# A new prologue for a hybrid attention and mLSTM layer: the order of its loads, tiles in pairs, and the low parts of h made by GpSimd

## The chip, the cores and the metric

The kernel runs on one core of one Trainium2 chip. The metric is the device time of one execution in microseconds, lower is better. The engines are TensorE (PE), VectorE (DVE), ScalarE (ACT), GpSimd (POOL) and SyncE (SP), which here only issues DMAs. Each engine runs its own instructions in order and waits on semaphores that others raise.

## The reference

One decoder layer, batch 1, sequence 1024, width 1024, all float32:

```
mod = silu(c) @ w_ada + b_ada;  shift, scale, gate = split(mod, 3)
h = x * (1 + scale) + shift
proj = h @ w_in + b_in      # 8 heads of stick-breaking attention: q k v z (4 x 512);
                            # 4 heads of mLSTM: q k v o z (5 x 512), i f (2 x 4); two merge gates (2 x 1024)
y_sb = (stick_breaking(q, k, v) * silu(z)) @ w_sb_proj
y_ml = (head_norm(mlstm(silu(conv(q, k)), v, i, log_sigmoid(f))) * sigmoid(o) * silu(z)) @ w_ml_proj
y = (sigmoid(g_sb) * y_sb + sigmoid(g_ml) * y_ml) @ w_out
out = layer_norm(alpha * x + (1 + gate) * y, ln_g, ln_b)
```

The prologue is the part that matters here: the conditioning `mod` (only shift and scale; 1024 x 2048 weights), `h`, and the first products with `w_in`.

## The kernel before, in words

h is kept transposed in SBUF: 8 tiles (d or k from 0 to 7), each of 128 channels on the partitions by 1024 tokens. To get float32 precision from the fast matmul mode (fp32r), every operand is split into a high and a low part, and a product is three matmuls: high by high, low by high and high by low (`split_product`, lines 614 to 619). So each tile of h exists as `hH` (a rounded copy) and `hL` (the rest). Weights are split in the same way, in chunks of four k tiles: ACT makes the high part (`wH` or `w_proH`) and DVE the low part (`wL` or `w_proL`).

The prologue goes over the 8 tiles, d = 0 to 7. For each tile:

- SP loads 128 columns of x (`x_rows`, line 453) and the 2 x 128 conditioning columns of `w_ada` (`a_raw`, line 457, three buffers). All loads of the prologue are on SP's one queue, in this order; the rows that they read are 512 bytes long. The small parameter rows (`prm`, seven loads) go ahead of all.
- DVE multiplies the eight 128-row blocks of `a_raw` with silu(c) and adds them up in two sums (`ada_rows`, lines 1323 to 1338: two TENSOR_SCALAR, six SCALAR_TENSOR_TENSOR, one addition, all 256 wide).
- PE sums over the partitions with two one-column matmuls by ones (`ada_columns`, line 655), and DVE adds the bias (`mod_columns`, lines 1366 and 1367): the shift and scale columns of the tile.
- PE transposes x (`turn_x`, line 667: two PSUM banks of four 128x128 transposes), ACT makes `h_raw` = x * scale + shift from the two banks (line 944) and copies it to `hH` (line 948). `h_raw` has two buffers. DVE makes `hL` = `h_raw` - `hH` (`low_h`, line 1360).
- PE multiplies the tile with the weights of jobs 0, 1 and 2 (`tile_of`): job 0 is the eight gate rows i and f (128x8 weights), in two PSUM banks; jobs 1 and 2 are q and k of the first pair of attention heads (128x128 weights). Each job is 6 matmuls of 512 columns in a tile: 2 halves of the tokens by 3 terms.

PE's order is written out by hand (lines 699 to 711): columns of tile 0; then for each d: transposes of x tile d, jobs 0 and 1 of tile d-1, columns of tile d+1, job 2 of tile d-1. After the last tile come jobs 3 and 4 (v and z of that pair), 48 matmuls each over all of h (`project`, line 639). Job 3 writes the PSUM banks of job 1, so it waits until ACT has copied jobs 0 and 1 out (`drained`). Then `gate_columns` (line 691) transposes rows made from the gates, and the main loop of four iterations begins.

Beside jobs 3 and 4 runs the chain of the gate rows. POOL zeroes four row buffers that lie where `x_rows` was (lines 563 to 567, `rows_zero`) once PE has transposed the last x. ACT copies job 0 out of PSUM with its bias to `r_if` (line 961). SP moves the rows by eight small DMAs to four partition groups (`r_f`, `r_i`, lines 470 and 472). Then ACT takes exponential and logarithm (lines 993, 995), DVE does two scans and builds `r_q` (lines 1388 to 1408), and ACT takes exponentials (line 1000). In DVE's order the low part of weight chunk 9 stands behind the scans (`row_logs`, `pro_split`).

POOL does nothing between its constants, which end at about 4 us, and the zeroing.

Of the kernel before, what the change touches and what calls it, by code (L numbers as in the profile page):

```python
# [25 lines left out]
P = 128  # L26
D = 1024
# [102 lines left out]
A_BUFS = 3  # L130
Y_BUFS = 4


# [64 lines left out]
def build_kernel(nc, x, c, w_ada, b_ada, w_in, b_in, conv_w, conv_b, ml_norm_g, w_sb_proj, w_ml_proj, w_out,  # L198
# [13 lines left out]
    with ExitStack() as ctx:  # L212
# [30 lines left out]
        next_v, next_g = lt("next_v", [P, S]), lt("next_g", [P, S])  # L243
# [39 lines left out]
        a_raw = pt("a_raw", [P, A_BUFS, KT, 2, P])  # L283
        a_acc = pt("a_acc", [P, 2, 2, 2, P])
# [3 lines left out]
        w_proH = pt("w_proH", [P, PRO_CHUNKS, 4, P], F32R)  # L288
        w_proL = pt("w_proL", [P, PRO_CHUNKS, 4, P], F32R)
# [31 lines left out]
        params_in, bias_in = sem("params_in"), sem("bias_in")  # L321
        x_cols_in = [sem(f"x_cols_in{d}") for d in range(KT)]
# [4 lines left out]
        ada_summed = sem("ada_summed")  # L327
        ada_used, ada_done, mod_done = sem("ada_used"), sem("ada_done"), sem("mod_done")
# [50 lines left out]
        pro_ps = [[y_ps[0:2 * NH, :], misc_ps[2][0:2 * NH, :]],  # L379
                  [proj_ps[half][:] for half in range(2)], [z_ps[half][:] for half in range(2)]]  # L380
        ada_ps = misc_ps[0]
# [16 lines left out]
        def banks(number):  # L398

            return z_ps if number > J_GATES and (number - J_GATES) % 2 else proj_ps  # L400

# [24 lines left out]
        def _(sp):  # L426
            bi = b_in[0]
            rows = [
                (ROW_C, c[0]), (ROW_ADA, b_ada[0]), (ROW_B, bi[0:OFF_IF]),
                (ROW_GSB, bi[OFF_GSB:OFF_GSB + 2 * D]), (ROW_CB, conv_b[0]), (ROW_NG, ml_norm_g[0]),  # L430
            ]
            for row, src in rows:
                src = src.rearrange("(t p) -> t p", p=P)
                sp.dma_start(prm[row:row + src.shape[0], :], src).then_inc(params_in, 16)
            sp.dma_start(prm[ROW_CW:ROW_CW + 4 * KT, :], conv_w[0].rearrange("j (t p) -> (j t) p", p=P))\
                .then_inc(params_in, 16)

# [13 lines left out]
            for d in range(KT):  # L451
                cols_d = slice(d * P, (d + 1) * P)
                sp.dma_start(x_rows[:, :, cols_d], x_v[:, :, cols_d]).then_inc(x_cols_in[d], 16)
                if d >= A_BUFS:
                    sp.wait_ge(ada_used, KT * (d - A_BUFS + 1))
                for what in range(2):
                    sp.dma_start(a_raw[:, d % A_BUFS, :, what], w_ada_w[:, :, what, cols_d])\  # L457
                        .then_inc(a_in[d % A_BUFS], 16)
# [1418 lines left out]
```

## Time and profile before

| | us |
|---|---|
| median of 3 runs (962.40 to 962.66) | 962.57 |
| the profiled execution's own time | 964.36 |
| its span, first to last instruction | 962.6 |
| PE busy (share of the span) | 931.1 (97%) |
| DVE busy | 616.4 (64%) |
| ACT busy | 440.4 (46%) |
| POOL busy | 165.5 (17%) |
| mean granted TensorE clock | 0.996 |

PE is the busy engine, and the chain that ended last lies on PE for 89% of the span. Matmuls are pipelined, so that a busy PE isn't PE at its peak; the record of a matmul is longer than the distance between two. Idle time of the other engines costs nothing by itself. The first 24 us are the only stretch in which PE is idle for long: its busy share is 2 tenths in the first of the page's 40 slices, and 9 or more in all the others.

### The profile page before, as it was taken

What the parts mean: (1) busy time and instruction counts of PE and PEld (TensorE: products, weight loads), DVE (VectorE), ACT (ScalarE), POOL (GpSimd) and SP (SyncE); (2) the same over time, 40 slices, a digit from 0 to 9 for tenths busy, and PEclk for the clock granted to TensorE, in tenths of its full rate; (3) what the DMA queues carried; (4) which work ended last, traced back from release to release, by engine and by line L of the source; (5) the groups of instructions that cost most, each with busy time, mean ns of one, the idle gap of its engine ahead of it and who ended that gap; (6) DMA issues with size and microseconds to landing.
All of it is one profiled execution on the core that took longest, in us unless ns stands there. A gap on an engine that the chain in (4) does not pass through costs nothing.

```text
span 962.6 us, 12901 instructions
## 1 busy us (share of the span) xinstructions
PE 931.1 (97%) x4965; PEld 759.7 (79%) x4965; DVE 616.4 (64%) x1112; ACT 440.4 (46%) x717; POOL 165.5 (17%) x114
## 2 busy tenths in 40 slices
PE   2999999999999999999999999999999999999996
PEld 1677878888878888788888888888888888878885
DVE  4756886755976647976649967534653333345996
ACT  2454566553666544575544665425743222242100
POOL 1010232220223230322311322211100000001200
PEclk9999999999999999999999999999999999999999
DMA  9941211112201022111112111127612212215232
GB/s 228 291 99 48 67 35 39 35 36 67 77 23 45 23 55 78 43 45 34 33 44 89 33 35 34 43 55 237 211 45 67 53 46 53 88 44 186 91 129 87
DMA packets 99560, 73.95 MB, mean 77 GB/s; under 512 B 4616, under 2 KB 90760, under 8 KB 99500
## 3 DMA queue, kind: packets, MB, share of 16 engines
q1 hardware_dynamic: 94828, 58.44, 22.7%
q0 software_dynamic: 2368, 8.41, 2.6%
q10 hardware_dynamic: 2304, 6.29, 1.8%
q8 instruction: 39, 0.64, 0.3%
q14 instruction: 21, 0.17, 0.1%
HBM read 64.59 MB, written 8.40 MB: 76 GB/s over the span
## 4 chain that ended last, share of the span: by engine, by line
PE 89%; DVE 4%; ACT 2%; SPq 2%; DMA 2%; issue 1%; DVEq 0%; ACTq 0%
PE bank L639 44%; PE bank L619 10%; PE bank L617 10%; PE bank L618 10%; PE bank L758 4%; PE bank L746 3%; PE bank L733 2%; DMA a_raw<-in_w_ada 2%; PE bank L716 2%; DVE rem L1503 1%; PE bank L735 1%; PE bank L734 1%; SPq L457 1%; PE bank L781 1%; PE bank L783 1%
## 5 line engine op out<-in xcount | busy, mean ns | idle before, releaser
L639 PE MATMUL bank<-hH,wH 128*128 128x512 f32 x688 | 271.1, 394 | 0.6 <-DVE wL L1343 0.6
L639 PE MATMUL bank<-hL,wH 128*128 128x512 f32 x688 | 271.2, 394 | 0.0
L639 PE MATMUL bank<-hH,wL 128*128 128x512 f32 x688 | 271.1, 394 | 0.0
L577 POOL TENSOR_TENSOR ez<-ez,rem 128x512 f32<-128x512 f32 x72 | 134.5, 1881 | 396.8 <-DVE rem L1503 396.8
L1343 DVE SCALAR_TENSOR_TENSOR wL<-w_raw,wH 128x512 fp32r<-128x512 f32 x116 | 99.3, 860 | 109.2 <-ACT wH L920 107.9
L639 PEld LDWEIGHTS bank<-hH,wH 128*128 128x128 f32 x688 | 129.3, 188 | 30.3 <-DVE wL L1343 2.1
L639 PEld LDWEIGHTS bank<-hH,wL 128*128 128x128 f32 x688 | 129.3, 188 | 28.8 <-issue 2.9
L639 PEld LDWEIGHTS bank<-hL,wH 128*128 128x128 f32 x688 | 129.2, 188 | 28.8 <-issue 2.9
L1503 DVE TENSOR_TENSOR_SCAN rem<-rem,ones 128x512 f32<-128x512 f32 (+2 forms) x96 | 99.9, 1093 | 35.1 <-ACT rem L1020 35.1
L920 ACT ACTIVATE wH<-w_raw 128x512 fp32r<-128x512 f32 x116 | 72.5, 627 | 104.3 <-PE bank L619 71.1
L1008 ACT ACTIVATE ez<-bank 128x512 f32<-128x512 f32 x72 | 39.1, 596 | 101.1 <-PE bank L735 101.1
L618 PE MATMUL bank<-hL,wH 128*128 128x512 f32 x144 | 56.2, 390 | 0.0
L617 PE MATMUL bank<-hH,wH 128*128 128x512 f32 x144 | 56.2, 390 | 0.0
L619 PE MATMUL bank<-hH,wL 128*128 128x512 f32 x144 | 56.0, 389 | 0.0
L606 POOL TENSOR_TENSOR yL<-yT,yH 128x1024 fp32r<-128x1024 f32 x4 | 9.6, 2402 | 207.5 <-ACT yH L1272 207.5
L1016 ACT ACTIVATE rem<-ez 128x512 f32<-128x512 f32 x72 | 41.4, 625 | 7.7 <-DVE y_stage L1510 6.1
L1020 ACT ACTIVATE rem<-rem 128x512 f32<-128x512 f32 x72 | 41.1, 621 | 0.0
L1027 ACT ACTIVATE at<-bank 128x512 f32<-128x512 f32 x72 | 38.7, 592 | 3.3 <-PE bank L746 3.3
L617 PE MATMUL bank<-hH,yH 128*128 128x512 f32 x96 | 38.5, 401 | 0.0
L618 PE MATMUL bank<-hL,yH 128*128 128x512 f32 x96 | 38.1, 396 | 0.0
L619 PE MATMUL bank<-hH,yL 128*128 128x512 f32 x96 | 38.0, 396 | 0.0
L746 PE MATMUL bank<-ident,ez 128*128 128x128 f32 x288 | 37.2, 272 | 0.0
(241 smaller groups left out, 1499.6 us busy)
## 6 DMA issues: line engine op xcount, KB each, us to landing
w_raw<-in_w_in SPq DMA_DIRECT2D x104, 256.0 KB, 2.9
a_raw<-in_w_ada SPq DMA_DIRECT2D x16, 512.0 KB, 7.3
x_rows<-in_x SPq DMA_DIRECT2D x8, 512.0 KB, 6.4
raw<-in_w_ada POOLq DMA_DIRECT2D x8, 512.0 KB, 4.8
x_in<-in_x SPq DMA_DIRECT2D x8, 512.0 KB, 4.2
out_y<-res SPq DMA_DIRECT2D x7, 512.0 KB, 2.9
raw<-in_w_out SPq DMA_DIRECT2D x10, 256.0 KB, 4.5
m_w<-bm_scratch ACTq DMA_DIRECT2D x4, 512.0 KB, 3.5
```

The source lines that it names most:

```text
L577: g.tensor_tensor(e, e, r, ALU.mult).then_inc(a_done[h], 1)
L617: t.matmul(ps, aH, bH, start=k == 0, stop=False)
L618: t.matmul(ps, aH, bL, start=False, stop=False)
L619: return t.matmul(ps, aL, bH, start=False, stop=k == kt - 1)
L639: ins = t.matmul(banks(number)[half][:], w, a, start=(r == 0), stop=(r == JOB_MM // 2 - 1))
L746: ins = t.transpose(z_ps[h][:, b * P:(b + 1) * P], ez[s % 2][h][:, b * P:(b + 1) * P], ident[:])
L920: a.activation(wH[:, slot, :, 0:width], w_raw[:, slot, :, 0:width], ACT.Copy, scale=scale)\
L1008: a.activation(ez[s % 2][h][:], z_ps[h][:], ACT.Exp).then_inc(ex_done[h], 1)
L1016: a.activation(rem[s % 2][h][:], ez[s % 2][h][:], ACT.Ln, bias=1.0).then_inc(ln_done[h], 1)
L1020: a.activation(r, r, ACT.Exp, scale=-1.0).then_inc(rem_done[h], 1)
L1343: v.scalar_tensor_tensor(out=wL[:, slot, :, 0:width], in0=w_raw[:, slot, :, 0:width], scalar=scale, in1=wH[:, slot, :, 0:width], op0=ALU.m ...
L1503: v.tensor_tensor_scan(back, back, ones[:, 0:1].to_broadcast((P, hi - lo)), first, ALU.mult, ALU.min).then_inc(scan_done[h], 1)
```

## The change

It touches the prologue alone, up to the copies of job 0 and the moves of its rows.

1. **Loads.** SP loads c and b_ada first, then the conditioning weights ahead of x. The tiles are in blocks [0], [1], [2, 3], [4, 5], [6, 7]: a block of two is loaded with rows of 1 KB, its weights in two pieces of four k blocks each. There are four buffers for pieces (`A_BUFS`), the fourth where `next_v` and `next_g` lie. The other parameter rows are loaded from ACT's queue, ahead of its table load. Weight chunks 3 to 5 are loaded after block 2.
2. **Conditioning.** DVE's row products are 512 wide for a block of two. Of its eight, ACT makes the first two (`ada_begin`), after the first tile of the block before (d = 0, 2, 4). PE makes all columns of the block at once, between jobs 1 and 2 of the tile ahead of the block, and DVE adds the bias to all in one instruction (the 1 is added to the scale's bias once).
3. **Turning x.** PE transposes x two tiles ahead: tile d+2 at the end of tile d. `ada_ps` moves to another bank, so that it no longer shares one with the transposes.
4. **Gate rows.** Job 0 is done in full float32, from `h_raw` and the raw weights, as two matmuls for each tile instead of six. Its two halves write partitions 0 to 7 and 32 to 39 of one PSUM bank, so they lie in different column groups of the array.
5. **Low parts of h.** `low_h` is on POOL, all eight before the zeroing.
6. **After the last tile.** ACT copies half 0 of job 0 with its bias; DVE copies half 1 from partitions 32 to 39 to its place (`if_moved`), and ACT adds the bias there. The four moves to `r_i` are issued from ACT's queue behind that, ahead of the copies of jobs 1 and 2; those to `r_f` stay on SP.

```diff
@@ SP
+            for b, tiles in enumerate(BLOCKS):
+                cols_b = slice(tiles[0] * P, (tiles[-1] + 1) * P)
+                for number, lo, hi in ada_pieces(b):
+                    if number >= A_BUFS:
+                        sp.wait_ge(ada_used, ada_freed(number))
+                    for what in range(2):
+                        sp.dma_start(ada_piece(number, lo, hi)[:, :, what], w_ada_w[:, lo:hi, what, cols_b])\
+                            .then_inc(a_in[number % A_BUFS], 16)
+                sp.dma_start(x_rows[:, :, cols_b], x_v[:, :, cols_b]).then_inc(x_cols_in[b], 16)
+                for g in {0: range(3), 2: range(3, PRO_CHUNKS)}.get(b, ()):
+                    pro_load(g)
...
-            for q in range(4):
-                sp.dma_start(r_i[32 * q:32 * q + NH, :], r_if[0:NH, :]).then_inc(rows_in, 16)
@@ POOL
+            def low_h(d):
+                pool.wait_ge(hH_done, d + 1)
+                g.tensor_tensor(hL[:, d], h_raw[:, d % 2], hH[:, d], ALU.subtract).then_inc(hL_done, 1)
+
+            for d in range(KT):
+                low_h(d)
             pool.wait_ge(m_filled[0], KT + 1)
             pool.wait_ge(m_filled[1], KT)
             for z in (r_i, r_f, r_if):
@@ PE
+            def gate_rows(d):
+                for n in range(2):
+                    pe.wait_ge(m_drained[n], d + 2 - n)
+                if d % 4 == 0:
+                    pe.wait_ge(wL_done, PRO_K * (d // 4) + 1)
+                for half in range(2):
+                    ins = t.matmul(pro_ps[0][half], w_if[:, d], h_raw[:, d % 2, halves(half)], start=d == 0,
+                                   stop=d == KT - 1, skip_group_check=True)
...
+            turn_x(0)
             ada_columns(0)
+            turn_x(1)
             for d in range(KT):
...
+                gate_rows(d)
+                tile_of(d, 1)
+                if d + 1 < KT and BLOCKS[BLOCK_OF[d + 1]][0] == d + 1:
+                    ada_columns(BLOCK_OF[d + 1])
+                tile_of(d, 2)
+                if d + 2 < KT:
+                    turn_x(d + 2)
@@ ACT
             def shifted(d):
-                act.wait_ge(mod_done, 2 * d + 2)
+                act.wait_ge(mod_done, BLOCK_OF[d] + 1)
                 if d > 1:
+                    act.wait_ge(if_used, d - 1)
                     act.wait_ge(hL_done, d - 1)
...
+            def ada_begin(b):
+                act.wait_ge(a_in[ada_pieces(b)[0][0] % A_BUFS], 32 * (ada_pieces(b)[0][0] // A_BUFS + 1))
+                act.wait_ge(silu_done, 1)
+                act.wait_ge(ada_done, b - 1)
+                for k in range(ada_first(b)):
+                    a.activation(ada_sum(b, k), ada_row(b, k), ACT.Copy, scale=silu_c[:, k:k + 1]).then_inc(ada_begun, 1)
...
             for d in range(KT):
                 shifted(d)
-                if d < 3:
-                    pro_split(d + 3)
+                if d in (0, 2, 4):
+                    ada_begin(d // 2 + 2)
+                if d == 3:
+                    for g in range(3, PRO_CHUNKS):
+                        pro_split(g)
...
+                if n == 0:
+                    for half in range(2):
+                        act.wait_ge(drained[half], 1)
+                    for q in range(4):
+                        act.dma_start(r_i[32 * q:32 * q + NH, :], r_if[0:NH, :]).then_inc(rows_in, 16)
@@ DVE
+            other_columns()
+            ada_rows(0, 0, KT)
+            mod_columns(0)
+            for g in range(3):
+                pro_split(g)
+            for b in range(1, len(BLOCKS)):
+                ada_rows(b, 0, KT // 2)
+                ada_rows(b, KT // 2, KT)
+                mod_columns(b)
+                if b == 3:
+                    for g in range(3, PRO_CHUNKS):
                         pro_split(g)
-            low_h(KT - 1)
+            dve.wait_ge(filled[1], 1)
+            dve.wait_ge(rows_zero, 5)
+            v.tensor_copy(r_if[0:2 * NH, halves(1)], pro_ps[0][1]).then_inc(if_moved, 1)
             for g in range(PRO_CHUNKS, PRO_CHUNKS + 3):
                 pro_split(g)
```

## Rows read from the trace of the kernel before

**Rows 1.** The page: busy us of the engines, share of the span, instructions

```profile
PE 931.1 (97%) x4965; PEld 759.7 (79%) x4965; DVE 616.4 (64%) x1112; ACT 440.4 (46%) x717; POOL 165.5 (17%) x114
```

**Rows 2.** Stretches: length, PE, PEld, DVE, ACT, POOL busy; clock, DMA share, GB/s

```profile
45.00:50.00 5.00, 5.00 (x23) 3.30 (x22) 3.77 (x11) 2.61 (x3) 0.00 (x0) 0.79 1.14 291
...
55.00:60.00 5.00, 5.00 (x27) 3.67 (x27) 4.17 (x13) 2.51 (x3) 0.00 (x0) 1.00 0.06 17
```

**Rows 3.** Timeline of DVE, 0 to 62 us: start, length, instruction, idle before

```profile
11.43 0.61 DVE L1331 TENSOR_SCALAR a_acc<-a_raw,silu_c 128x256 f32<-128x256 f32 x2 [4.28 <-DMA a_raw<-in_w_ada]
...
16.05 0.15 DVE L1367 SCALAR_TENSOR_TENSOR mod<-bank,cols 128x1 f32<-128x1 f32 x1
...
23.32 0.15 DVE L1367 SCALAR_TENSOR_TENSOR mod<-bank,cols 128x1 f32<-128x1 f32 x1
...
55.45 0.15 DVE L1367 SCALAR_TENSOR_TENSOR mod<-bank,cols 128x1 f32<-128x1 f32 x1
...
60.96 0.15 DVE L1367 SCALAR_TENSOR_TENSOR mod<-bank,cols 128x1 f32<-128x1 f32 x1
```

**Rows 4.** Timelines of DVE, POOL, ACT, SP and PE, 60 to 77 us

```profile
65.26 1.23 DVE L1360 TENSOR_TENSOR hL<-h_raw,hH 128x1024 fp32r<-128x1024 f32 x1 [4.15 <-ACT hH L948]
...
63.08 0.95 POOL L564 MEMSET r_i<- 128x1024 f32 x1 [58.30 <-PE bank L667]
...
66.77 0.11 POOL L567 MEMSET r_one<- 128x8 f32 x1
...
67.94 1.28 ACT L961 ACTIVATE r_if<-bank,r_bias 8x512 f32<-8x512 f32 x2 [1.16 <-PE bank L619]
...
76.09 1.06 ACT L993 ACTIVATE r_e<-r_f 128x1024 f32<-128x1024 f32 x1 [4.05 <-DMA r_i<-r_if]
...
69.33 2.55 SPq L470 DMA_DIRECT2D r_f<-r_if  x4
...
71.15 0.39 PE L639 MATMUL bank<-hH,wH 128*128 128x512 f32 x1
```

**Rows 5.** PE's timeline at 85.5 us, and the chain that ended last, there

```profile
85.52 0.50 PE L639 MATMUL bank<-hH,wH 128*128 128x512 f32 x1 [0.58 <-DVE wL L1343]
...
85.52 8.48 PE bank L639 x36
```

**Rows 6.** Timeline of SP's DMA issues: the first load of x

```profile
3.48 0.43 SPq L453 DMA_DIRECT2D x_rows<-in_x  x1
```

**Rows 7.** Timeline of PE around its pause at 41 us, and later

```profile
41.82 0.61 PE L655 MATMUL bank<-ones,a_acc 128*128 128x1 f32 x4 [1.52 <-DVE a_acc L1337]
...
43.86 1.91 PE L667 MATMUL bank<-ident,x_rows 128*128 128x128 f32 x8
...
46.42 0.63 PE L619 MATMUL bank<-hH,w_proL 128*8 128x512 f32 x1
...
50.89 1.04 PE L667 MATMUL bank<-ident,x_rows 128*128 128x128 f32 x8
```

**Rows 8.** Groups, 0 to 72 us: shapes, count, busy us, mean ns, idle before

```profile
L944 ACT ACTIVATE h_raw<-bank,mod 128x512 f32<-128x512 f32 x16 | 11.9, 776 | 29.0 <-PE bank L667 29.0
...
L948 ACT ACTIVATE hH<-h_raw 128x1024 fp32r<-128x1024 f32 x8 | 8.5, 1061 | 0.7
...
L1352 DVE SCALAR_TENSOR_TENSOR w_proL<-w_raw,w_proH 128x512 fp32r<-128x512 f32 x4 | 2.6, 682 | 0.0
```

**Rows 9.** Line 606 on POOL: ns min/median/max, first and last start

```profile
L606 POOL TENSOR_TENSOR yL<-yT,yH x4: 2400/2402/2403, 875.7 to 909.7; 128x1024 fp32r<-128x1024 f32 x4
```

**Rows 10.** Timeline of POOL and DVE around 188 us

```profile
187.64 3.87 POOL L577 TENSOR_TENSOR ez<-ez,rem 128x512 f32<-128x512 f32 x2 [9.08 <-DVE rem L1503]
...
188.65 1.71 DVE L1343 SCALAR_TENSOR_TENSOR wL<-w_raw,wH 128x512 fp32r<-128x512 f32 x1
```

**Rows 11.** Timeline of PE: full float32 matmuls (each recorded twice)

```profile
862.99 1.88 PE L877 MATMUL bank<-g_acc,ones 128*128 128x512 f32 x4
...
130.68 1.09 PE L758 MATMUL bank<-at,v_tok 128*64 128x128 f32 x16
```

More of the change, by code:

```diff
@@ L129, with pro_slot, ada_pieces, ada_first @@
 PRO_CHUNKS = 2 * PRO_K
-A_BUFS = 3
+A_BUFS = 4
+BLOCKS = [[0], [1], [2, 3], [4, 5], [6, 7]]
+BLOCK_OF = [b for b, tiles in enumerate(BLOCKS) for _ in tiles]
 Y_BUFS = 4
+def pro_slot(g):
+    return (g // PRO_K) * (PRO_K - 1) + g % PRO_K - 1
+def ada_pieces(b):
+    if b < 2:
+        return [(b, 0, KT)]
+    return [(2 * b - 2 + part, part * KT // 2, (part + 1) * KT // 2) for part in range(2)]
+def ada_first(b):
+    return 0 if b < 2 else 2
+def ada_steps(b, k):
+    return sum(KT - ada_first(x) for x in range(b)) + max(k - ada_first(b), 0)
+def ada_freed(number):
+    return [ada_steps(b, hi) for b in range(len(BLOCKS)) for n, _, hi in ada_pieces(b) if n == number - A_BUFS][0]
 def segments():
@@ L426, in _ @@
         def _(sp):
[L427 to L436, printed above, removed]
+            sp.dma_start(prm[ROW_C:ROW_C + KT, :], c[0].rearrange("(t p) -> t p", p=P)).then_inc(c_in, 16)
+            sp.dma_start(prm[ROW_ADA:ROW_ADA + 3 * KT, :], b_ada[0].rearrange("(t p) -> t p", p=P)).then_inc(c_in, 16)
             def load(slot, src, split):
@@ L979, in _ @@
                             act.wait_ge(rows_zero, 5)
-                        bias_copy(r_if[0:2 * NH, halves(half)], half, n,
-                                  r_bias[0:2 * NH, :], pro_ps[0][half])
+                        else:
+                            act.wait_ge(if_moved, 1)
+                        rows = r_if[0:2 * NH, halves(half)]
+                        bias_copy(rows, half, n, r_bias[0:2 * NH, :], rows if half else pro_ps[0][half])
                     elif n < 4:
@@ L1370, in _, with mod_columns @@
-            for d in range(KT):
-                ada_rows(d)
-                if d:
-                    low_h(d - 1)
-                mod_columns(d)
-                if d == 0:
-                    for g in range(3):
+            def mod_columns(b):
+                dve.wait_ge(ada_done, b + 1)
+                first, tiles = BLOCKS[b][0], len(BLOCKS[b])
+                bias = cols[:, ROW_ADA:ROW_ADA + 2 * KT].rearrange("p (w d) -> p w d", w=2)[:, :, first:first + tiles]
+                v.tensor_tensor(mod[:, :, first:first + tiles],
+                                ada_ps[:, 0:2 * tiles].rearrange("p (w d) -> p w d", w=2), bias, ALU.add)\
+                    .then_inc(mod_done, 1)
```

180 lines of the change are left out of this document (96 added, 84 removed).

## The prediction

> **What bounds the kernel now.** I read the page first: TensorE (PE) is busy for 931.1 of 962.6 us [rows 1]. So a change can gain only in the 31 us in which PE idles or runs at its lower clock, and the prologue holds most of them. Next, the table by stretches: the transfers run at 291 GB/s from 45 to 50 us and have ended by 55 (17 GB/s), the granted clock is 0.79 between 45 and 50 us, and PE is full by then [rows 2]. Third, VectorE's (DVE's) timeline: the conditioning columns of the first tile of h exist at 16.2 us, and those of the last two tiles come at 55.6 and 61.1, 5.51 us apart [rows 3]. That interval is PE's own work for one tile, since PE has no gap there. Fourth, the end of the prologue [rows 4]: hL of tile 7 is ready at 66.5, the zeroing on GpSimd (POOL) ran from 63.08 to 66.88, before the gate rows were there, ScalarE (ACT) copies them out from 67.94, and PE goes on without a gap to job 3 at 71.15. Last, the only later stall that the prologue causes: PE waits 0.58 us at 85.5 for weights whose low part stands behind the scans on DVE; and 36 matmuls in 8.48 us make 0.236 us for each [rows 5].
>
> So the number that counts is the start of job 3, now 71.15. After it come 22 us of pure projection, with the row chain beside them, and none of that changes in length.
>
> **The start.** The conditioning weights are issued at about 1.6 us, behind two small parameter loads of 0.4 each, instead of at 3.9 behind seven and 512 KB of x [rows 6]. Before, 1.5 MiB issued from 3.48 were there at 11.43: 7.9 us, of which 5.4 are transfer at 290 GB/s and 2.5 latency. Now 1 MiB from 1.6 takes 3.6 + 2.5, so it is there at 7.7. The columns exist 4.8 us after the landing (11.43 to 16.20 [rows 3]): 12.5 instead of 16.2. The parameter rows, now on ACT's queue, land by then; nothing waits for them.
>
> **The first two tiles.** Tile 1's weights have 3 MiB in all before them: 1.6 + 2.5 + 10.8 = 14.9, and its x is there at 16.7. PE turns that x before it does tile 0 (1.9 us at the low clock [rows 7]), then the gate rows (1.0), one 128-column part of tile 0 (six matmuls: 1.4 at full clock, 2.6 at the low one) and the columns (1.0, and 0.2 for DVE): 22.2 to 23.5. Today they come at 23.5 [rows 3]. The early start is used up here.
>
> **The step for one tile.** ACT makes h_raw in two pieces and hH: two of 0.72 or so, and 1.06, 2.5 us [rows 8]. POOL makes hL. The nearest operation is POOL's subtraction of the same shape, 2.40 us [rows 9]; DVE did it in 1.23 [rows 4]. After it PE does a part (1.4 to 2.6), then the next columns (0.7 to 1.4 with DVE's sum). So the columns of pair 2, 3 come 7.0 to 8.9 us after those of tile 1: 29.2 to 32.4.
>
> **The cadence of a pair.** The next pair's columns stand on PE behind the part of the second tile of this pair. By that way a pair costs h_raw and hH (2.5), the two first products that ACT now makes between the two tiles (512 wide, half of hH's 1.06 and a start-up: about 2 x 0.6), h_raw and hH again (2.5), hL (2.4), the part (1.4), columns (0.8), and some 0.4 for semaphores: 11.2 us. Today two tiles cost 2 x 5.51 = 11.0. The pairs make DVE cheaper (one operation of 0.68 [rows 8] for two narrower ones), but DVE isn't what sets this chain: hL, ACT's extra products and PE's order are in it.
>
> A second way is longer if POOL and DVE can't work at once. In the trace a DVE operation that takes 0.68 us elsewhere [rows 8] takes 1.71 when it is issued beside POOL's [rows 10]. DVE then starts its products when hL of the first tile is done, 5.0 us after the columns, needs 6 x 0.66 + 0.7 = 4.7, stands once more for 2.4, and the columns take 0.8: 12.9 us. The Trainium skill (SBUF — State Buffer, "SBUF: two separate sides") says why: the port pair is "an exclusive lock, not a bandwidth split", and a DVE operation with two SBUF inputs wants it. By that rule the pair costs 12.9, without it 11.2; rows 10 agree with the rule. I take 12.1 for each of the two pairs, between the ends, because the second stand may fall where DVE has already finished.
>
> **The end of h.** After the last pair's columns come 2.5 + 2.5 on ACT and 2.4 on POOL, 7.6 with semaphores. hL of tile 7 is then ready at 29.2 + 22.4 + 7.6 = 59.2 at best and 32.4 + 25.8 + 7.6 = 65.8 at worst, or 68 if PE's pauses keep the clock low for much of the time. I take 64.5. That is only 2 us before today's 66.5. Faster transfers don't help: even at 290 GB/s the last piece, the 13th MiB after 1.6, is there at about 51, when the chain wants it near 52. Wider rows can only bring it earlier.
>
> **The gate rows.** Six fast matmuls become two in full float32. Two such matmuls of 512 columns took 1.88 us to the end of the last, and eight of 128 columns that alternate between halves of the array's columns took 1.09 [rows 11]; the first is the bound if they run one after the other, the second, scaled by four quarters of a pair (some 1.0), if side by side. The skill (TensorEngine Tiling (Array Packing), "Key Properties") says that tiles work in parallel; by that 1.0 instead of 1.4, else 1.7. Either is hidden while the chain waits for ACT and POOL, but for up to 0.7 us at the end. I take 1.0.
>
> **What stands behind the last hL.** This is where I expect the loss. POOL does all eight hL first and zeroes its rows only then. The zeroing takes 3.8 us (63.08 to 66.88 [rows 4]) and was hidden; now it begins at the end of hL 7. Behind it stand, one after the other: ACT's copy of one half of the gate rows (0.65; DVE moves the other beside it), ACT's bias on the other (0.65), four DMA issues that this ACT queue now makes (SP made four such in 2.55 [rows 4]; at 0.43 each, as for x [rows 6], 1.7), and the copy of job 1's first half (0.65). Only then may job 3 write its bank. That is 8.3 us, or 7.5 with quick issues. Job 3 thus starts at 64.5 + 8.3 = 72.8, against 71.15: +1.65.
>
> PE has finished tile 7 by 68.3 (hL at 64.5, with the gate row and 2.8 us behind it) and stands for some 4 us. After a pause of 1.5 us today's clock fell for a while: eight transposes took 1.91 instead of 1.04, and matmuls 0.63 us instead of the usual 0.40 until about 47 [rows 4, 7]. That pause cost 0.87 + 4 x 0.23 = 1.8 us, and I put nearly the same on job 3: +1.7 (from 0 to 2.4).
>
> **The row chain.** The moves to r_f wait on SP behind the load of chunk 9, which waits for a split behind DVE's new copy: issued at hL + 5.5, landed at hL + 10.4 = 74.9, while ACT began on them at 76.09 today [rows 4]. It gains 1.2 while PE loses 3.3, so the 0.58 stall goes: -0.6. Nothing else becomes late; the transposed gate columns follow 17 us after that landing, at 92, and PE wants them at 97.
>
> **Sum.** +1.65 + 1.7 - 0.6 = +2.75. The profiled execution took 964.36, 1.8 more than the median shown, so 967.1 for such an execution and **965.3** against the median 962.57.
>
> **Rivals.**
> (a) *Neutral, 0.25.* The clock doesn't fall, or hL 7 comes at 62.5: job 3 at 70.8 + 1.7 - 0.6, so 963.3.
> (b) *Faster, 0.2.* The place is the chain of pairs: at 11.2 us, with pair 2, 3 at 29.2, hL 7 is there at 59.2 and job 3 at 67.5. That is -3.65 - 0.6 + 1.7 = -2.55, 960.0 (958.3 without the clock's part). For it speaks that PE, DVE and the transfers all have room; against it, the low clock and rows 10. It decides from hL 7 before 59.9: at 61.8 the change breaks even, at 59.9 it gains 0.2%.
> (c) *The lock decides, 0.2.* Both pairs at 12.9 and low clock in most pauses: hL 7 at 67.5, job 3 at 75.8, +4.65 + 1.7 - 0.6: 968.3. The skill's exclusive lock alone gives 65.8 and 966.6.
> (d) *It doesn't do what it says, 0.02.* POOL's hL takes over 3 us, as its 512-wide multiplications beside DVE took 1.9 each [rows 10] and not half of 2.4: over 970.
>
> The forecast itself has 0.33, between 964.5 and 967. A measurement of this kernel can tell 0.2% (1.9 us) from no change. Faster by more than that: (b), 0.2. Within: (a) and a little of the forecast, 0.27. Slower: 0.53. The range from 959.5 to 969.5 leaves out the ends of (b) and of (c) with (d).
>
> **What would show it.** Right: columns of tile 0 at 12.4 and of the last pair at 52 to 58; pairs 11 to 13 us apart; the zeroing straight behind the last hL; PE idle 3 to 5 us ahead of L639's first matmul, released by ACT's next_q copy, and a granted clock below 1 there; no wait for wL at job 4. Wrong: hL 7 before 60, or job 3 without a gap behind tile 7, or a DVE that isn't slowed beside POOL.

## The result: 967.4 us, 5.0 us slower

| | before | after |
|---|---|---|
| median (us) | 962.40 (962.27 to 962.66, 5 runs) | 967.36 (967.34 to 971.06, 5 runs) |
| the profiled execution, and its span | 964.36, 962.6 | 967.36, 965.6 |

The ratio of the means is 1.0062, 95% interval 1.0046 to 1.0078 (so are the ratios below). The forecast was 965.3 (959.5 to 969.5), slower the likeliest with 0.53; the measured time lies in that range, and just outside the band of 964.5 to 967 in which the forecast itself was to hold. In the profiled executions the span grew by 3.0 us, and my sum said 2.75; the rest of the difference lies in the profile of before, as will be shown.

The busy time of the page, the line that answers to [rows 1]:

```profile
PE 930.6 (96%) x4950; PEld 756.2 (78%) x4950; DVE 612.5 (63%) x1061; ACT 443.5 (46%) x723; POOL 185.5 (19%) x122
```

PE does the same work as before. POOL has 20 us more: eight low parts of 2.3 to 2.8. DVE has only 4 us less, although it gave up eight low parts of 1.23. Its timeline says why; it answers to [rows 3] (start, length, instruction; in brackets the idle time before it and who ended it):

```profile
12.64 0.16 DVE L1462 TENSOR_TENSOR mod<-bank,cols 128x2 f32<-128x2 f32 x1 [1.11 <-PE bank L699]
23.53 0.16 DVE L1462 TENSOR_TENSOR mod<-bank,cols 128x2 f32<-128x2 f32 x1 [2.94 <-PE bank L699]
31.78 0.16 DVE L1462 TENSOR_TENSOR mod<-bank,cols 128x4 f32<-128x4 f32 x1 [1.27 <-PE bank L699]
35.32 7.67 DVE L1432 SCALAR_TENSOR_TENSOR a_acc<-a_raw,silu_c,a_acc 128x512 f32<-128x512 f32 x6 [3.38 <-ACT a_acc L1023]
44.86 0.16 DVE L1462 TENSOR_TENSOR mod<-bank,cols 128x4 f32<-128x4 f32 x1 [1.14 <-PE bank L699]
57.95 0.16 DVE L1462 TENSOR_TENSOR mod<-bank,cols 128x4 f32<-128x4 f32 x1 [1.15 <-PE bank L699]
```

The `mod` rows are the ends of the blocks' columns. The early start is there (12.8 for 16.2), by tile 1 it is used up (23.7 for 23.5), and the pairs come 13.1 us apart where two single tiles took 2 x 5.51 (31.78, 44.86 and 57.95). Between two `mod` rows the chain can be read off: DVE waits 3.38 us for ACT (h_raw, hH and the two begun products), then its six products take 7.67, then the sum and the columns. Two such products took 1.41 at 23.64 us, where POOL is idle, so six take some 4.1 (an estimate); here they take nearly twice that, beside two of POOL's low parts (34.66 to 37.01 and 38.37 to 41.13).

POOL, PE, ACT, its queue and SP's at the end of the prologue, and after it, answering to [rows 4] (the first row of PE is the first product of tile 4):

```profile
34.66 2.35 POOL L594 TENSOR_TENSOR hL<-h_raw,hH 128x1024 fp32r<-128x1024 f32 x1 [5.41 <-ACT hH L1015]
38.37 2.76 POOL L594 TENSOR_TENSOR hL<-h_raw,hH 128x1024 fp32r<-128x1024 f32 x1 [1.36 <-ACT hH L1015]
61.17 4.86 POOL L594 TENSOR_TENSOR hL<-h_raw,hH 128x1024 fp32r<-128x1024 f32 x2 [6.97 <-ACT hH L1015]
69.66 0.11 POOL L604 MEMSET r_one<- 128x8 f32 x1
...
50.14 0.50 PE L654 MATMUL bank<-hH,w_proH 128*128 128x512 f32 x1 [1.96 <-POOL hL L594]
...
63.56 0.77 PE L654 MATMUL bank<-hH,w_proH 128*128 128x512 f32 x1 [2.30 <-POOL hL L594]
64.14 0.63 PE L655 MATMUL bank<-hL,w_proH 128*128 128x512 f32 x1
68.10 1.03 PE L721 MATMUL bank<-h_raw,w_if 128*8 128x512 f32 x4
74.95 0.47 PE L676 MATMUL bank<-hH,wH 128*128 128x512 f32 x1 [2.83 <-ACT next_q L1040]
96.79 1.03 PE L747 MATMUL bank<-ident,r_q 128*128 128x128 f32 x8
...
69.94 0.68 ACT L1040 ACTIVATE r_if<-bank,r_bias 8x512 f32<-8x512 f32 x1 [4.81 <-POOL r_one L604]
71.40 2.67 ACTq L1076 DMA_DIRECT2D r_i<-r_if  x4
74.12 1.27 ACT L1040 ACTIVATE next_q<-bank,cols 128x512 f32<-128x512 f32 x2 [2.80 <-issue]
78.21 1.06 ACT L1079 ACTIVATE r_e<-r_f 128x1024 f32<-128x1024 f32 x1 [1.67 <-DMA r_f<-r_if]
91.86 3.22 ACT L1086 ACTIVATE r_q<-r_q 32x1024 f32<-32x1024 f32 x3 [4.54 <-DVE r_q L1503]
...
71.68 2.74 SPq L503 DMA_DIRECT2D r_f<-r_if  x4
```

The last hL ends at 66.0, the zeroing behind it at 69.8, the gate rows' copies run from 69.94, the four issues of r_i take 2.67, next_q follows, and PE, idle for 2.83 us, starts job 3 at 74.95. The row L747, at 96.79, is a good mark for what follows: in before's profile the same transposes (L691 there) stood at 93.84, and from that mark to the end of the span both kernels take 868.8 us. So the mark alone tells what the prologue and the row chain (the gate rows' way to `r_q`) cost, and I use it for the other profiled executions too.

The stretches (columns as in [rows 2]):

```profile
30.00:45.00 15.00, 12.81 (x70) 8.94 (x69) 9.18 (x11) 7.29 (x11) 5.10 (x2) 1.00 1.10 349
60.00:70.00 10.00, 7.70 (x27) 4.43 (x26) 0.13 (x1) 5.07 (x8) 8.40 (x7) 0.83 0.01 2
70.00:80.00 10.00, 7.17 (x32) 5.61 (x31) 2.36 (x4) 5.50 (x8) 0.00 (x0) 1.00 0.41 92
```

From 50 to 60 us the transfers are at 1 GB/s, so they bound nothing at the end. The granted clock fell behind the pause of 2.30 us ahead of tile 6 (matmuls of 0.63) and stayed at 1.00 behind the pause at job 3. That fall did cost PE time: it came to tile 7 at 69.06, 3 us after hL 7. But the copies of the gate rows had to wait for POOL's zeroing until 69.8 in any case, so the fall did not move job 3.

### The profile page after: what moved, and what is told of

It is laid out like the page before. It is cut to its first block, busy times and chain, and to the rows that moved or that the text cites. A ratio compares the mean times of both kernels' runs of the same rounds, so it can differ in the third digit from the quotient of the medians.

```text
span 965.6 us, 12851 instructions
## 1 busy us (share of the span) xinstructions
PE 930.6 (96%) x4950; PEld 756.2 (78%) x4950; DVE 612.5 (63%) x1061; ACT 443.5 (46%) x723; POOL 185.5 (19%) x122
## 3 DMA queue, kind: packets, MB, share of 16 engines
q1 hardware_dynamic: 85380, 58.32, 21.9%
## 4 chain that ended last, share of the span: by engine, by line
PE 88%; DVE 4%; ACT 3%; POOL 1%; issue 1%; SPq 1%; DMA 1%; ACTq 0%; DVEq 0%; POOLq 0%
PE bank L676 46%; PE bank L654 9%; PE bank L656 9%; PE bank L655 9%; PE bank L815 4%; PE bank L803 3%; PE bank L790 2%; PE bank L773 2%; DVE a_acc L1432 1%; DVE rem L1603 1%; PE bank L792 1%; PE bank L791 1%; POOL hL L594 1%; DMA x_rows<-in_x 1%; PE bank L838 1%
```

## The experiments

Four theories had to be told apart (the letters in the expectations are those of each expectation alone). **A**: POOL's low parts cost the time, by their length and by stretching DVE's products. **B**: what stands behind the last hL (zeroing, issues on ACT's queue) costs it. **C**: the new prologue is at fault even without POOL. **D**: PE's pauses cost it, through the clock.

### The low parts on DVE again

```diff
-            for d in range(KT):          # on POOL
-                low_h(d)
...
                 ada_rows(b, 0, KT // 2)  # on DVE
+                low_h(BLOCKS[b - 1][0])
-                ada_rows(b, KT // 2, KT)
+                ada_rows(b, KT // 2, KT - 2)
+                for d in BLOCKS[b - 1][1:]:
+                    low_h(d)
+                ada_rows(b, KT - 2, KT)
...
+            for d in BLOCKS[-1]:
+                low_h(d)
```

> The changed kernel with the eight low parts of h back on DVE (1.2 us each, between the row products); all else as changed. Theory A (the low parts on POOL are the loss: 2.4 us instead of 1.2 in the chain of each pair, DVE held beside them, and the zeroing behind the last): pairs 11.2 to 11.8 us apart instead of 13.1, hL 7 near 61.5 instead of 66.0, the zeroing at 60 to 64 and hidden, job 3 at 67.5 to 68.5 instead of 74.95, so about 960 us against 967.4 and below the kernel before. Theory B (the loss is only what stands behind the last tile, ACT's DMA issues above all): the pairs stay 12.5 or more apart and the time falls by at most 2 us, to 965.5 or more.

967.83 us (966.33 to 970.98, 6 runs), ratio 1.0058 (1.0045 to 1.0071): no gain. The products are short again, but PE's timeline shows a new wait:

```profile
37.47 0.50 PE L648 MATMUL bank<-hH,w_proH 128*128 128x512 f32 x1 [2.83 <-DVE hL L1462]
52.50 0.80 PE L648 MATMUL bank<-hH,w_proH 128*128 128x512 f32 x1 [2.83 <-DVE hL L1462]
```

The low part of a pair's first tile stands behind two products that wait for ACT's two. PE pauses for 2.83 us, the granted clock falls (0.66 from 50 to 60 us), PE's matmuls take 0.63, and now PE is the limit of the chain: the pairs' columns come 15.0 and 16.2 us apart. What the edit gave was taken by its order. It doesn't yet speak against A.

### Low parts on DVE, the first one ahead of the products

```diff
+                if b > 2:
+                    low_h(BLOCKS[b - 1][0])
                 ada_rows(b, 0, KT // 2)
-                low_h(BLOCKS[b - 1][0])
+                if b < 3:
+                    low_h(BLOCKS[b - 1][0])
```

> The low parts of h are made on VectorE again, as in the run with both on VectorE, but for the blocks of pairs the first tile's low part stands ahead of all products of the next block, so that it doesn't stand behind products that wait for ScalarE's two. Theory C (PE's pause ahead of a pair's first tile decides, since a long pause is followed by a low clock and PE then becomes the limit of the pairs): the pause ahead of tiles 2, 4 and 6 falls from 2.8 to about 0.8 us, the granted clock stays above 0.95 in 40:70, columns of the pairs come 11 to 12 us apart, the last hL is ready at 61 to 62 and job 3 starts at 68 to 70: 959 to 961 us. Theory D (VectorE's added 1.22 us a tile is itself what sets the pairs, wherever it stands): the pairs stay 13 us apart or more, and the time is 965 to 968.

962.93 us (961.04 to 964.14, 11 runs) beside 962.67 for before, ratio 0.9999 (0.9990 to 1.0008).

```profile
34.78 1.23 DVE L1462 TENSOR_TENSOR hL<-h_raw,hH 128x1024 fp32r<-128x1024 f32 x1 [2.66 <-ACT hH L1009]
44.07 0.16 DVE L1456 TENSOR_TENSOR mod<-bank,cols 128x4 f32<-128x4 f32 x1 [2.23 <-PE bank L693]
55.48 0.16 DVE L1456 TENSOR_TENSOR mod<-bank,cols 128x4 f32<-128x4 f32 x1 [1.52 <-PE bank L693]
...
48.18 0.50 PE L648 MATMUL bank<-hH,w_proH 128*128 128x512 f32 x1 [0.79 <-DVE hL L1462]
69.12 0.47 PE L670 MATMUL bank<-hH,wH 128*128 128x512 f32 x1 [2.16 <-ACT next_q L1034]
```

The low part uses time in which DVE is idle anyway (2.66 us). The pause ahead of tile 4 is 0.79, the pairs come 12.1 and 11.4 us apart, hL 7 is ready at 62.4, job 3 starts at 69.12. Theory C of the expectation (the pause decides) had these right, but for hL 7 by 0.4; its total, 959 to 961, was too good. The row at 69.12 says where it went: 2.16 us of pause for next_q are left, behind ACT's issues, and the clock falls behind them (0.83 from 70 to 80 us). One reordering of a 1.2 us instruction was worth 4.9 us against the run before.

### The clock by itself

In the first of these two kernels 40 transposes of `ident` that nobody reads were put on PE in each of the two long pauses:

```diff
                 gate_rows(d)
+                if d in (2, 4):
+                    for n in range(40):
+                        t.transpose(misc_ps[2][:, 3 * P:4 * P], ident[:], ident[:])
                 tile_of(d, 1)
```

> The run with the low parts on VectorE in the first order (967.8 us, pauses of TensorE of 2.8 us ahead of tiles 2 and 4, clock 0.66 in 50:60), with 40 transposes of ident that nobody reads in each of the two pauses; some 2.2 to 4.5 us each, by 0.06 to 0.11 us a transpose. Everything else stays. If the low clock behind the pause is what made the pairs 15 and 16 us apart, the clock stays at 1.00 in 30:60, the pairs come 13 to 13.5 us apart although TensorE has more to do, and the time falls by 2 to 4 us. If the late low parts alone did it, the pairs stay 15 us apart and the time is the same or 1 to 3 us more.

969.38 us (one execution; the kernel without them: 968.69 when profiled). PE's timeline, the fill and what follows:

```profile
35.24 4.58 PE L756 MATMUL bank<-ident 128*128 128x128 f32 x40
39.58 0.48 PE L648 MATMUL bank<-hH,w_proH 128*128 128x512 f32 x1
50.12 4.59 PE L756 MATMUL bank<-ident 128*128 128x128 f32 x40
```

The clock stays at 1.00 from 40 to 60 us, and no matmul there takes 0.63. But I filled too much: the first product starts 7.6 us after the pair's columns (31.99 and 46.87) where it started 6.15 after them behind the pause, so the pairs are 14.9 us apart. By its letter it is the second theory of the expectation that came out, pairs 15 us apart and a time not lower; the total is no evidence either way, for up to job 3 this execution is 0.8 us ahead (75.39 for 76.22), and then the clock falls behind the pause at job 3, which it had not done without the fill (0.83 from 70 to 80 us; 23.4 us to the mark for 21.9). The distance from a pair's first product to the next pair's columns is free of that: 37.47 to 46.35 and 52.50 to 62.6 (8.9 and 10.1 us) with the pause, 39.58 to 46.87 and 54.46 to 61.74 (7.3 and 7.3) with the fill. So the low clock cost 1.6 and 2.8 us a pair, and the pause itself 2.0 (2.83 for 0.79): with the 11.4 of the good order, 15.0 and 16.2, as measured. **D** is shown for this order of DVE's work, by one execution of each kernel. It is not what the changed kernel lost by: there the pauses of 1.95 us ahead of tiles 2 and 4 were followed by no fall, and the fall at tile 6 was hidden.

### No products on ACT

```diff
 def ada_first(b):
-    return 0 if b < 2 else 2
+    return 0
-                if d in (0, 2, 4):
-                    ada_begin(d // 2 + 2)
```

> The changed kernel with all eight row products of a pair on DVE, none on ACT between its two tiles. Theory A (the serial chain through ACT holds DVE back: it stands 3.4 us for ACT's products after the columns, and ACT starts the second tile 1.2 us later for them): pairs 11.5 to 12 us apart instead of 13.1, so job 3 at 72 and 964.5 to 965.5 us. Theory B (DVE's own work beside POOL is the limit): with two products more on DVE the pairs are 13 to 14 us apart and the time is the same or up to 1.5 us higher.

973.40 us (971.46 to 973.84, 4 runs), ratio 1.0107 (1.0092 to 1.0121). DVE now starts at once, and its products are stretched further:

```profile
33.65 8.29 DVE L1430 SCALAR_TENSOR_TENSOR a_acc<-a_raw,silu_c,a_acc 128x512 f32<-128x512 f32 x6
47.52 0.16 DVE L1460 TENSOR_TENSOR mod<-bank,cols 128x4 f32<-128x4 f32 x1 [4.85 <-PE bank L699]
```

DVE finished its sum before PE could want it (4.85 us idle). The pairs were 14.7 us apart all the same: POOL's low part came 0.5 to 0.6 us later behind the columns, PE paused for 2.55 and 2.48 us, and the clock fell to 0.83 from 40 to 60. Neither theory of the expectation came out. ACT's two products are worth 6 us in this order, and 2.6 of these are a fall of the clock behind a pause of 4.38 us at job 3 (24.4 us from there to the mark, 21.8 in the changed kernel).

### What POOL does to DVE: two subtractions, or five memsets, more

```diff
             for d in range(KT):
                 low_h(d)
+                if d < KT - 2:
+                    for n in range(2):
+                        pool.wait_ge(idle_step, 2 * d + n)
+                        g.tensor_tensor(idle_out[:], sel_all[:], sel_all[:], ALU.subtract).then_inc(idle_step, 1)
```

and in the other kernel five `g.memset(idle_out[:], 0.0)` in their place.

> The changed kernel, and behind each of the first six low parts GpSimd makes two more subtractions of 128x512 elements that nothing reads (about 1.2 us each). They end before the next tile's hH is there or shortly after, so by GpSimd's own time they cost at most 1 us in all. If GpSimd's reads of SBUF hold VectorE's products up for as long as they last (the lock), the products of a pair are stretched by another 2 to 4 us, the pairs' columns come 15 to 17 us apart instead of 13.1, and job 3 starts 5 to 10 us later. Without the lock the products keep 7.67 us for six and job 3 stays at 75 to 77.

> The changed kernel with five memsets of 128x512 on GpSimd behind each of the first six low parts, as long as the two subtractions were that stretched the products and cost 8 us, but reading nothing from SBUF. If it is GpSimd's reads of SBUF that VectorE's products collide with, the products stay as in the changed kernel (7.67 us for six of 128x512) and the time is 967 to 968.5. If any work of GpSimd does it, the products are stretched as by the subtractions and the time is 972 to 976.

With the subtractions 975.27 us and pairs 16.3 and 16.2 us apart, as the lock's theory had it, with the memsets 969.56 and 13.2 (one execution each). POOL's and DVE's timelines, first with the subtractions:

```profile
36.78 2.93 POOL L604 TENSOR_TENSOR idle_out<-sel_all 128x512 f32<-128x512 f32 x2
...
35.14 10.79 DVE L1439 SCALAR_TENSOR_TENSOR a_acc<-a_raw,silu_c,a_acc 128x512 f32<-128x512 f32 x6 [3.38 <-ACT a_acc L1030]
```

then with the memsets:

```profile
36.50 2.87 POOL L604 MEMSET idle_out<- 128x512 f32 x5
...
34.88 7.64 DVE L1439 SCALAR_TENSOR_TENSOR a_acc<-a_raw,silu_c,a_acc 128x512 f32<-128x512 f32 x6 [3.38 <-ACT a_acc L1030]
...
66.31 1.03 PE L728 MATMUL bank<-h_raw,w_if 128*8 128x512 f32 x4
...
74.73 0.77 PE L683 MATMUL bank<-hH,wH 128*128 128x512 f32 x1 [4.38 <-ACT next_q L1047]
```

Equal lengths on POOL, and only one of them stretches DVE: 7.64 is what the changed kernel itself shows (7.67). So it is not POOL's being busy that holds up DVE's two-input products. What the subtractions do and the memsets don't is to read from SBUF; they are another operation as well, which these two runs don't separate. The Trainium skill (SBUF — State Buffer, "SBUF: two separate sides") has the lock, for a DVE operation with two SBUF inputs, "only against a GpSimd op that reads SBUF", and the two rows agree. The total of the memset run was 1.1 to 2.6 us more than I expected of this outcome, and its cause is another: job 3 starts even earlier (74.73), but here the clock fell behind that pause (0.66 from 70 to 80 us). It may be what happened in the changed kernel's own runs of 968.94 and 971.06; those have no profile, only a mean clock of 0.994 and 0.991 for 0.996. At tile 6 the clock did not fall here, although PE paused for 2.31 us, and the gate rows end at 67.3 and not at 69.1.

### POOL's low parts alone, in the kernel before

```diff
-                if d:                    # on DVE
-                    low_h(d - 1)
-            low_h(KT - 1)
+            for d in range(KT):          # on POOL, ahead of the zeroing
+                low_h(d)
```

> The kernel before with one edit: GpSimd makes the low parts of h, nothing else is changed. VectorE is rid of 8 times 1.22 us, GpSimd takes 2.3 to 2.6 us for each, and they share a port as far as VectorE's two-operand products go. Theory A (the move of the low parts by itself costs time, whatever the order around it): the last hL comes at 68 to 69 us instead of 66.5, the zeroing behind it ends at 72 to 73, job 3 starts 2 to 4 us later, 964 to 967 us. Rival (VectorE's relief shortens the block by more than the hL lengthens it): columns come less than 5.4 us apart and the time is 962 or below.

970.92 us (970.05 to 971.12, 4 runs), ratio 1.0083 (1.0070 to 1.0097): 8.3 us, more than I gave it.

```profile
67.45 2.40 POOL L563 TENSOR_TENSOR hL<-h_raw,hH 128x1024 fp32r<-128x1024 f32 x1 [3.11 <-ACT hH L954]
...
43.07 2.45 DVE L1343 TENSOR_TENSOR a_acc<-a_acc 128x256 f32<-128x256 f32 x1
...
75.63 0.47 PE L645 MATMUL bank<-hH,wH 128*128 128x512 f32 x1 [1.38 <-ACT next_q L967]
91.21 0.50 PE L645 MATMUL bank<-hH,wH 128*128 128x512 f32 x1 [1.74 <-DVE wL L1349]
```

The sum at 43.07 took 2.45 us beside a low part, 0.42 elsewhere. The last hL is there at 69.85, and the mark stands at 99.51. With an undisturbed clock the prologue of before has its last hL at 64.9 (that execution is shown at the end of the section on the prediction), and its mark would stand at 91.9, 93.84 less the 1.9 us that the low clock took. So the mark moved by 7.6: 5.0 up to the last hL, and 2.6 behind it (the zeroing, the pause for next_q, the wait for wL). Of the 5.0, 3.4 are there at the last columns, above all by DVE's operations stretched at tiles 1 and 4, and 1.5 come with the last tile, 1.2 of them by the low part's own length.

### Behind the last hL

Two edits of the changed kernel, the second on top of the first: SP issues the moves of r_i behind those of r_f, and DVE zeroes the rows (`v.memset`, while it is idle from 60.8 us on).

```diff
-                        act.dma_start(r_i[32 * q:32 * q + NH, :], r_if[0:NH, :]).then_inc(rows_in, 16)
+                sp.dma_start(r_i[32 * q:32 * q + NH, :], r_if[0:NH, :]).then_inc(rows_in, 16)
...
-                g.memset(z[:], 0.0).then_inc(rows_zero, 1)   # the second kernel
+                v.memset(z[:], 0.0).then_inc(rows_zero, 1)
```

> The changed kernel with the four moves to r_i issued by SP behind those to r_f, as in the kernel before; ACT then copies job 1 out right behind the gate rows. Theory A (PE's wait for job 3 is the issues' 2.7 us, and nothing is given back): job 3 at 72.1 instead of 74.95, the time 2.8 us lower, 964.6. Theory B (what PE gains, it loses at job 4): the moves land some 1 us later, near 79, the scans end later, and PE waits 2 to 3 us for the low part of chunk 9 in job 4; the time changes by less than 0.7 us.

> The kernel of e2 with the zeroing of the four row buffers on DVE, which is idle from 58 us, instead of behind the last low part on POOL. If the zeroing is on the path: job 3 starts straight behind tile 7 at 72.0, the gate rows are copied out at 69.1 instead of 69.9, the moves land 0.8 us earlier than in e2, so the wait in job 4 is 1.8 us rather than 2.6: about 0.8 us below e2, 1 to 1.3 below the changed kernel. If only the issues count: the same as e2.

966.74 us (966.55 to 968.18, 5 runs), ratio 1.0050 (1.0038 to 1.0062), and 966.19 (964.35 to 967.49, 5 runs), ratio 1.0037 (1.0025 to 1.0049). PE after the prologue, in the first:

```profile
87.68 0.50 PE L678 MATMUL bank<-hH,wH 128*128 128x512 f32 x1 [1.96 <-DVE wL L1438]
```

The pause of 2.83 us ahead of job 3 is gone in both, and 1.96 of it, in the second 1.44, come back at job 4, where the low part of a weight chunk stands behind DVE's two scans. The mark moves by 0.8 and 1.2. The zeroing itself is worth 0.4: with hL 7 at 66, PE's gate rows end at 69.1, so that most of it lies beside them. They end so late only because the clock fell at tile 6, in these two kernels as in the changed one (0.83 from 60 to 70 us). In the memset run, without that fall, they end at 67.3 and the zeroing at 69.6, so there it holds the copies up by 2.2. **B** is right in kind and small in size, and the smallness of the zeroing is in part the clock's.

Then both places at once: POOL's queue moves r_i, and the low part of the tenth chunk stands between the scans. With it ACT's exponential waits for r_f's four moves alone, and DVE's second scan for r_i's. These two edits were put on three kernels.

```diff
+            for q in range(4):                  # on POOL, behind the zeroing
+                pool.dma_start(r_i[32 * q:32 * q + NH, :], r_if[0:NH, :]).then_inc(ri_in, 16)
...
-                    act.wait_ge(rows_in, 16 * 8)
+                    act.wait_ge(rows_in, 16 * 4)
...
                 link.k += 1                     # behind the first scan
+                pro_split(PRO_CHUNKS + 3)
+                dve.wait_ge(ri_in, 16 * 4)
                 link(v.tensor_tensor_scan(r_m[:], r_f[:], r_i[:], 0.0, ALU.add, ALU.max))
```

On the changed kernel:

> The changed kernel (low parts of h on GpSimd) with the two edits behind the prologue that the run at 959.5 us has: r_i moved by GpSimd's queue, the tenth chunk's low part between the scans. Set beside that run, it tells what GpSimd's low parts cost once everything behind them is equal; set beside 967.4 us, what the two edits give there. Theory (low parts on GpSimd cost by their 1.3 us more on the path, by the lock on VectorE's products and by the zeroing behind them): 963.5 to 965 us, 4 to 5.5 above the run with VectorE's in good order; job 3 starts at 71.5 to 72.5 with no pause. Rival (the two edits alone made the gain, GpSimd or VectorE being equal): 960 us.

967.44 us (966.96 to 970.74, 5 runs), ratio 1.0060 (1.0047 to 1.0073). Nothing gained, against my 963.5 to 965:

```profile
78.19 1.06 ACT L1079 ACTIVATE r_e<-r_f 128x1024 f32<-128x1024 f32 x1 [4.90 <-DMA r_f<-r_if]
91.83 3.21 ACT L1086 ACTIVATE r_q<-r_q 32x1024 f32<-32x1024 f32 x3 [7.70 <-DVE r_q L1505]
...
95.10 1.09 PE L752 MATMUL bank<-ident,r_q 128*128 128x128 f32 x8 [1.31 <-ACT r_q L1086]
97.55 0.63 PE L681 MATMUL bank<-hL,wH 128*128 128x512 f32 x1
```

No pause at job 3, none at job 4; but now PE waits at the mark itself, 1.31 us, for the end of the row chain (gate rows, r_f's transfer, exp and ln, scans, r_q), and the clock falls behind it: eight matmuls 0.43 apart instead of 0.23, 1.6 us. In the changed kernel and the three made of it by edits behind the last hL (SP's issues, DVE's zeroing, and these two edits) the chain runs from the copy at 69.3 to 69.9 to the end of r_q at 94.7 to 95.1. The changed kernel's PE came 1.7 us behind that; with the chain as it is, more than 1.7 was not to be had on PE's side.

On the kernel before:

> The kernel before with the same two edits behind the prologue and its own prologue unchanged. It tells how much of the 3.2 us that the best run gains is the new prologue's. The trace of before has one pause of 0.58 us for wL there, and r_i's issues stand on SP where nobody waits: 961.8 to 962.2 us, so that 2.3 to 2.7 us are left to the prologue in its good order. Rival (the row chain behind the prologue is on the path, and moves up by the second set of issues as well): 960 us or less, and the prologue is worth at most 0.5.

961.87 us (961.49 to 962.33, 11 runs), ratio 0.9992 (0.9983 to 1.0001), as expected.

On the kernel with DVE's low parts in the good order:

> The kernel of the run before this one, and two more edits: the four moves of r_i are issued by GpSimd, which is free then, and no longer by ScalarE ahead of the copies of next_q; and VectorE's low part of the tenth weight chunk stands between the two scans, not behind both. If the end of the gate rows' chain is what remains after the prologue: no pause of PE at job 3 and none for wL at job 4, 2 to 3 us less than that kernel, 956 to 959 us. If GpSimd's queue lands r_i later than the second scan wants it, that scan waits, and the gain is 1 us or less.

**959.46 us** (959.28 to 959.85, 6 runs), ratio 0.9968 (0.9956 to 0.9980): 3.5 us less than without the two edits, just above the 956 to 959 that I expected, and the one version whose interval lies below the kernel before.

```profile
43.45 0.16 DVE L1456 TENSOR_TENSOR mod<-bank,cols 128x4 f32<-128x4 f32 x1 [1.52 <-PE bank L698]
54.86 0.16 DVE L1456 TENSOR_TENSOR mod<-bank,cols 128x4 f32<-128x4 f32 x1 [1.52 <-PE bank L698]
...
88.68 1.09 PE L746 MATMUL bank<-ident,r_q 128*128 128x128 f32 x8 [0.59 <-ACT r_q L1080]
```

The mark stands at 88.68, 8.1 us before the changed kernel's. Here too the row chain ends last, by 0.59.

The medians together (us):

| | low parts on DVE | low parts on POOL |
|---|---|---|
| prologue of before | 962.6 | 970.9 |
| the same, and the two edits behind it | 961.9 | not run |
| new prologue (on DVE: the good order) | 962.9 | 967.4 |
| the same, and the two edits behind it | 959.5 | 967.4 |

**A** is shown, against DVE's good order: in each row with both cells POOL's low parts cost 4.5 to 8.3 us. Against DVE's first order they cost nothing (967.8), so where DVE's low parts stand counts as much. The last row is the cleanest, and its 8.0 us can be followed: on POOL the last hL is 4.0 us later (65.7 for 61.7), the copy of the gate rows 6.2 (69.63 for 63.42; the clock's fall at tile 6 and the zeroing), the mark 6.4, and the low clock behind the mark adds 1.6.

**C** falls, with a condition: with POOL the new prologue gains 3.5 us, and with DVE in the good order and the edits it gains 2.4. Without the edits it gains nothing with DVE (962.9), and in the first order it loses 5.3.

## Why the prediction was right, and where it was off

1. **The start and the first two tiles**: 12.5 and 22.2 to 23.5 forecast, 12.8 and 23.7 measured. The first pair was said to come at 29.2 to 32.4; it came at 31.9. Right; the last pair's, said for 52 to 58, came at 58.1.
2. **The cadence of a pair**: 12.1 taken, between 11.2 without the lock and 12.9 with it. It took 13.1. The middle between the ends was the wrong choice, and "the second stand may fall where DVE has already finished" the wrong reason: DVE began only 3.38 us after the columns, when it had ACT's two products, so both low parts of a pair fell on its own six. The run with subtractions and the one with memsets show that this stretches them. But the 11.2 was wrong as well, and by more. PE's first product of a pair comes 5.3 us after the pair's columns (44.86 to 50.14), and behind it PE has 7.3 us of its own work before the next columns (48.18 to 55.48 in the good order, without a pause): jobs 1 and 2 of that tile, the turn of x, the next gate rows and job 1 of the pair's second tile. My way went through ACT and POOL to the second tile's low part and left this out; that low part was ready before PE came to it (38.37 + 2.76 for 41.88). So even without the lock these rows give 12.6 (an estimate), and the stretch added 0.5: 5.3 and 7.8 make 13.1. Against the good order, 4.1 and 7.3, a pair lost 1.2 by the low part's own length and 0.5 by the stretch. The lock's way gave 12.9 and would have put hL 7 at 65.8; it was there at 66.0, where I had 64.5. The 64.5 itself was above my own terms: the middles of 29.2 to 32.4, of two pairs and the 7.6 make 62.6, and I gave no term for the rest.
3. **Gate rows**: 1.0 taken; the record says 1.03, and the next matmul starts 0.96 after the first.
4. **Behind the last hL**: 8.3 us forecast to job 3, 8.9 measured (66.0 to 74.95), link by link as described, the four issues 2.67 for 2.55. But I put the loss on the zeroing in first place, and DVE's zeroing gained only 0.4, since PE's gate rows ended only at 69.1, behind the low clock at tile 6.
5. **The clock at job 3**: +1.7 forecast, 0 in the profiled execution, where it fell at tile 6 instead and was hidden. PE stood for 2.83 us and not for some 4, as it came to tile 7 late. The price itself was near (1.6 us at the mark in the last experiment on the changed kernel, 2.4 at job 3 in the memset run), its place was not.
6. **The stall at job 4** went, as forecast: -0.6. The slack of the row chain was 1.7 us and not the 5 I gave it: r_f was in use at 78.2 and not at 74.9, since hL 7 came 1.5 later and the four transfers were done 3.8 us after their last issue. Where the transfers of r_i were issued last, in the kernel before and in the run with SP's issues, that took 1.7. What delays them stays open: the next weight chunk is issued right behind the last move in all three (74.41, 76.59, and 74.47 here), so that alone doesn't explain it.

Terms 2 and 4 added 2.1 us to job 3 and term 5 took 1.7 back; so the sum of 2.75 met 3.0 by errors that cancelled, and that is luck. One reading at the start was wrong too: the 31 us outside of PE's busy time are idle time alone; what the low clock takes lies inside the busy time.

**The step that failed** is the last one of the sum, from the profiled execution to the median. I wrote that the profiled execution took 1.8 us more than the median and took that to be there in both kernels alike. It was not. The median of after is its profiled time. Before's profiled execution held a stretch at the clock 0.79, from its pause of 1.52 us at 41.82 [rows 2, 7], which I had read and even priced at 1.8. The run with the unchanged prologue and the two edits behind it shows the same prologue without it (PE's and DVE's timelines, and one stretch):

```profile
41.31 0.61 PE L658 MATMUL bank<-ones,a_acc 128*128 128x1 f32 x4 [0.65 <-DVE a_acc L1340]
...
59.40 0.15 DVE L1370 SCALAR_TENSOR_TENSOR mod<-bank,cols 128x1 f32<-128x1 f32 x1
...
40.00:50.00 10.00, 9.35 (x53) 6.99 (x52) 7.87 (x22) 3.21 (x5) 0.00 (x0) 1.00 1.16 292
```

The pause is 0.65, the clock 1.00, and the last columns come at 59.6 instead of 61.1. Fifteen runs of before have spans of 960.5 to 961.3, none 962.6. Against the usual execution the mark of after is 4.9 us later (96.79 for 93.84 less 1.9), and that is the measured 5.0. Rival (c), the lock with low clock, had 968.3 for a chance of 0.2, and the lock alone 966.6. Both were nearer than the forecast, but both had the same 1.8 taken off; without that they are 970.1 and 968.4, and the forecast is 967.1. So their nearness says nothing for them.

## What to carry to other kernels

Before work is moved to GpSimd, look at what VectorE does in the same microseconds: here two-input products beside a GpSimd operation that reads SBUF were stretched by most of the time that both were at work (3.6 of 4.5 us), and the moved instruction itself took twice as long. Then look at what stands on TensorE behind the moved result: its own length counts there in full. Where an engine waits anyway, a short instruction costs nothing ahead of the wait and microseconds behind it. Before a profiled execution's time is carried over to a median, look for a stretch that only that execution has, above all at the lower clock, and take it out of before alone.

## What the runs showed of the hardware

- Six 128x512 two-input products on DVE took some 4.1 us free of POOL (an estimate from 1.41 for two), 7.67 beside POOL's 128x1024 subtractions, 10.79 with two 128x512 subtractions more behind each of these, and 7.64 with five memsets in their place. POOL's subtraction itself went from 2.35 to 2.76 or 2.85.
- The granted clock did not follow the length of a pause alone. It stayed at 1.00 behind 2.83 us (the changed kernel, job 3) and 2.31 (the memset run, tile 6) and fell behind 2.16 (DVE in the good order, job 3), 1.52 (the kernel before, at 41.82) and 1.31 (the mark at 95.10); behind 4.38 (the memset run, job 3) it was 0.66 over the next stretch. Each fall cost 1.6 to 2.8 us.
- Loads in rows of 1 KB ran at 349 GB/s, in rows of 512 bytes at 291 and 292 (the kernel before and the one with the two edits).
- A DMA issue of 4 partitions (16 KB) took 0.58 to 0.70 us on SP's and ACT's queue, the first one of x 0.43; the same on POOL's queue took 2.07 us for four.
